# ACT counts three of the seven score tiles in the last 23 rounds of a top-k threshold search

## The reference

```python
s_idx = relu(einsum('bqhd,bkd->bqhk', qi, kidx) * (IDX_DIM ** -0.5))
score = einsum('bqhk,bqh->bqk', s_idx, w) * (IDX_HEADS ** -0.5)
score = where(mask, score, -inf)
top_val, top_idx = lax.top_k(score, topk)      # topk = 256
s = einsum('bqhd,bqkhd->bqhk', q, k[top_idx]) * (B_HEAD_DIM ** -0.5)
```

## Time and profile before

| | us |
|---|---|
| median of 3 runs | 1895.09 |
| lowest and highest | 1891.09, 1896.43 |
| the profiled execution | 1891.44 |
| its span, first to last instruction | 1889.7 |
| PE busy | 1727.5 |
| DVE busy | 1225.5 |
| ACT busy | 550.7 |
| POOL busy | 302.6 |

### The profile page before, as it was taken

The page is one execution under the profiler, slowest core; times in us unless marked ns, Lnnn a source line. Parts: engine busy times, 40 slices in busy tenths (PEclk is TensorE's granted clock), DMA queues, the critical chain, the costliest instruction groups (busy, mean ns, idle before and its releaser), DMA issues. The chain is left out here.

```text
span 1889.7 us, 21531 instructions
## 1 busy us (share of the span) xinstructions
PE 1727.5 (91%) x7518; PEld 1141.1 (60%) x7538; DVE 1225.5 (65%) x2668; ACT 550.7 (29%) x1055; POOL 302.6 (16%) x389
## 2 busy tenths in 40 slices
PE   6999999999688899999769999999996888999997
PEld 4566666788445456666345666667884454566663
DVE  3379999999754445554133799999997544455550
ACT  2286411000232233333023754200002322333330
POOL 2003422000111322211110033220001013211111
PEclk9999999999889999999979999999998899999999
DMA  5100010100502010000061000101105020000000
GB/s 170 48 23 23 23 45 23 45 24 22 195 1 90 18 40 23 23 23 23 22 181 48 23 23 23 45 25 43 45 1 195 1 89 25 32 24 23 23 23 34
DMA packets 21183, 86.26 MB, mean 46 GB/s; under 512 B 4512, under 2 KB 9120, under 8 KB 16224
## 3 DMA queue, kind: packets, MB, share of 16 engines
q1 hardware_dynamic: 21088, 84.99, 12.9%
HBM read 66.84 MB, written 18.14 MB: 45 GB/s over the span
## 5 line engine op out<-in xcount | busy, mean ns | idle before, releaser
L1235 PE MATMUL ps<-r_xn,r_w 128*128 128x384 f32 (+1 forms) x1824 | 587.2, 475 | 12.3 <-issue 7.8
L1235 PEld LDWEIGHTS ps<-r_xn,r_w 128*128 128x128 f32 x1824 | 346.7, 192 | 207.3 <-issue 21.1
L1063 DVE TENSOR_SCALAR_CACHE_REDUCE r_ix<-r_sc,smi 128x384 bf16<-128x384 f32 x434 | 405.4, 998 | 2.2
L1156 DVE TENSOR_REDUCE sm<-ps 128x1 f32<-128x384 f32 (+8 forms) x216 | 174.4, 812 | 175.1 <-PE ps L1370 87.0
L899 ACT ACTIVATE r_sc<-ps,sm 128x384 f32<-128x384 f32 (+8 forms) x216 | 169.8, 787 | 368.0 <-DVE sm L1156 367.2
L1302 PE MATMUL ps<-r_w,r_xn 128*128 128x256 f32 (+1 forms) x1152 | 251.3, 380 | 0.0
L1302 PEld LDWEIGHTS ps<-r_w,r_xn 128*128 128x128 f32 (+1 forms) x1152 | 211.4, 184 | 39.7 <-issue 5.0
L1364 PE MATMUL ps<-r_qk,r_ix 128*128 128x128 f32 (+4 forms) x608 | 157.1, 391 | 31.2 <-POOL r_ix L680 26.6
L1400 PE MATMUL ps<-r_vg,r_w 128*128 128x64 f32 (+1 forms) x1184 | 155.7, 276 | 21.7 <-DVE r_w L528 11.9
L1400 PEld LDWEIGHTS ps<-r_vg,r_w 128*128 128x128 f32 (+1 forms) x1184 | 144.6, 193 | 39.1 <-DVE r_w L491 21.7
L1364 PEld LDWEIGHTS ps<-r_qk,r_ix 128*128 128x128 f32 (+1 forms) x608 | 104.0, 197 | 88.2 <-issue 69.5
(11 more groups left out here) (175 smaller groups left out, 1721.4 us busy)
## 6 DMA issues: line engine op xcount, KB each, us to landing
r_w<-w_in SPq DMA_DIRECT2D x28, 1024.0 KB, 4.8
r_xn<-w_out SPq DMA_DIRECT2D x2, 4096.0 KB, 13.0
y<-r_res SPq DMA_DIRECT2D x16, 512.0 KB, 2.9
o_k<-r_qk SPq DMA_DIRECT2D x4, 1088.0 KB, 15.8
r_vg<-x SPq DMA_DIRECT2D x8, 512.0 KB, 10.0
r_xn<-ckT SPq DMA_DIRECT2D x2, 2048.0 KB, 7.9
r_xn<-vcache SPq DMA_DIRECT2D x2, 2048.0 KB, 13.8
o_v<-r_vg SPq DMA_DIRECT2D x4, 1024.0 KB, 17.8
```

The lines of the kernel that those rows point to most:

```text
L1063: ins = vec.tensor_scalar(unsel[t][0:rows(t), :], sc[t][0:rows(t), :], b, None, ALU.is_ge, ALU.add, accum_out=cnt[0:rows(t), c:c + 1])
L1156: vec.tensor_reduce(negm[0:r, c:c + 1], on_slot(s, w, r), X, ALU.max, negate=True)\
L1235: ins = nc.tensor.matmul(on_ring(key, cn), w[:, k, P * s + at:P * (s + 1) + at], xnT[:, k, c0:c0 + cn], start=(k == 0), stop=(k == KT - 1))
```

## The change

The tiles 6, 7 and SAMPLE (`ACT_TILES`, widths 896, 1024 and 1088) are counted by ACT in the 23 rounds of the third loop. ACT takes sign(candidate - score) over the row and sums it: below minus above. With equal values giving 0, the sum is at most `width - 512` when at least 256 scores are not below the candidate, up to the case of a score equal to it, for which `settle` makes one exact count on DVE at the candidate plus one and corrects the result. DVE counts the other four tiles, then waits for ACT's three counts (`act_counted`), compares them with `limit` in a step of its own, and goes on as before. ACT waits for each round's candidate (`cand_ready`). ACT's counts are steps of the same list as the drains: the first stands behind the 23rd projection piece after the index scores, the others behind the next 22 pieces.

```diff
+ACT_TILES = [6, 7, SAMPLE]
+DVE_TILES = [t for t in SCORED if t not in ACT_TILES]
+ND = len(DVE_TILES)
+NS = len(SCORED)
+COUNTS_AT = list(range(23, 23 + SPLITS[2]))
...
+        if done in COUNTS_AT:
+            new.append(("count", COUNTS_AT.index(done)))
...
     for u in UNITS[10:]:
         for g in range(len(TMG)):
             steps.append(("tm", u, g))
+            done += 1
+            steps += after_piece(done)
...
+                    def count_out(n):
+
+                        act.wait_ge(cand_ready, n + 1)
+                        for t in ACT_TILES:
+                            c, r = SCORED.index(t), rows(t)
+                            nc.scalar.activation(unsel[t][0:r, :], sc[t][0:r, :], ACT.Sign, scale=-1.0,
+                                                 bias=cb.bitcast(f32)[0:r, c:c + 1],
+                                                 accum_out=cnt[0:r, c:c + 1]).then_inc(act_counted, 1)
...
-                    def count(bound, last_inc):
-                        for c, t in enumerate(SCORED):
+                    def count(bound, tiles):
+                        for t in tiles:
+                            c = SCORED.index(t)
...
+                    for t in ACT_TILES:
+                        c = SCORED.index(t)
+                        vec.memset(limit[:, c - ND:c - ND + 1], float(width(t) - 2 * TOPK))
+                    vec.memset(maskf[:, 0:1], 65535.0)
+                    vec.memset(maskf[:, 1:2], 2147418112.0)
+                    link(vec.memset(maskf[:, 2:3], 65536.0))
+                    link(vec.tensor_copy(maski, maskf))
+                    link(count(0.0, SCORED))
...
+                    def search_shared(rounds):
+                        base, first = steps[0], 0
+                        per = 4
+                        with dve.Fori(0, rounds) as i:
+
+                            vec.scalar_tensor_tensor(cb, v, bitv, smask, ALU.bitwise_or, ALU.bitwise_xor)\
+                               .then_inc(cand_ready, 1)
+                            dve.wait_ge(cand_ready, i + (first + 1))
+                            count(cb.bitcast(f32), DVE_TILES).then_inc(dve_step, 1)
+                            dve.wait_ge(dve_step, i * per + (base + 1))
+                            vec.tensor_scalar(kb[:, 0:ND], cnt[:, 0:ND], float(TOPK), bitf, ALU.is_ge, ALU.mult)
+                            dve.wait_ge(act_counted, i * len(ACT_TILES) + len(ACT_TILES) * (first + 1))
+                            vec.tensor_tensor(kbf, cnt[:, ND:NS], limit, ALU.is_le).then_inc(dve_step, 1)
+                            dve.wait_ge(dve_step, i * per + (base + 2))
+                            vec.tensor_scalar(kb[:, ND:NS], kbf, bitf, None, ALU.mult).then_inc(dve_step, 1)
+                            dve.wait_ge(dve_step, i * per + (base + 3))
+                            vec.tensor_tensor(v, v, kb, ALU.bitwise_or)
...
+                    def settle():
+
+                        va, sa = v[:, ND:NS], smask[:, ND:NS]
...
+                        link(vec.tensor_tensor(cb[:, ND:NS], two, sa, ALU.bitwise_xor))
+                        link(count(cb.bitcast(f32), ACT_TILES))
+                        link(vec.tensor_scalar(ca, cnt[:, ND:NS], float(TOPK), -1.0, ALU.is_ge, ALU.mult))
...
-                    search(SPLITS[2])
+                    search_shared(SPLITS[2])
+                    settle()
```

More of the change, by code:

```diff
@@ L324, in build @@
         bitv = smi[:, 28:29]
+        limit, kbf, maskf = sm[:, 224:227], sm[:, 228:231], sm[:, 232:235]
+        sti = sb("sti", 16, i32)
+        maski = smi[:, 29:32]
         lamjunk = sb("lamjunk", CHALF)
@@ L369, in build @@
         sel_ready = sem("sel_ready")
+        cand_ready, act_counted = sem("cand_ready"), sem("act_counted")
         lam_s, lam_e, lam_ready = sem("lam_s"), sem("lam_e"), sem("lam_ready")
@@ L874, in _ @@
                             nc.scalar.activation(tall, tall, ACT.Sqrt, scale=-1.0).then_inc(root_ready, 1)
+                        elif s[0] == "count":
+                            count_out(s[1])
                         elif s[0] == "iw":
@@ L1072, in _ @@
                     vec.memset(v, 0)
-                    link(count(0.0, None))
+                    for t in ACT_TILES:
[6 more added lines that the diff above has]
+                    link(count(0.0, SCORED))
                     link(vec.tensor_scalar(smask, cnt, float(TOPK), -1.0, ALU.is_lt, ALU.mult))
@@ L1083, in search @@
                             dve.wait_ge(dve_step, i * per + (base + 1))
-                            count(cb.bitcast(f32), None).then_inc(dve_step, 1)
+                            count(cb.bitcast(f32), SCORED).then_inc(dve_step, 1)
                             dve.wait_ge(dve_step, i * per + (base + 2))
@@ L1092, in search @@
                         steps[0] = base + per * rounds
+                    def search_shared(rounds):
[14 more added lines that the diff above has]
+                            vec.tensor_tensor(v, v, kb, ALU.bitwise_or)
+                            vec.tensor_scalar(bitv, bitf, 0.5, None, ALU.mult)
+                            vec.tensor_scalar(bitf, bitf, 0.5, None, ALU.mult).then_inc(dve_step, 1)
+                            dve.wait_ge(dve_step, i * per + (base + 4))
+                        steps[0] = base + per * rounds
@@ new lines, in settle @@
+                    def settle():
+                        va, sa = v[:, ND:NS], smask[:, ND:NS]
+                        low, high, one, two, ca = (sti[:, 3 * q:3 * q + 3] for q in range(5))
+                        m16, mhi, carry = (maski[:, q:q + 1].to_broadcast([P, 3]) for q in range(3))
+                        link(vec.tensor_tensor(low, va, m16, ALU.bitwise_and))
+                        link(vec.tensor_scalar(low, low, 1.0, None, ALU.add))
+                        link(vec.tensor_tensor(one, low, carry, ALU.bitwise_and))
+                        link(vec.tensor_tensor(low, low, m16, ALU.bitwise_and))
+                        link(vec.tensor_tensor(high, va, mhi, ALU.bitwise_and))
+                        link(vec.tensor_tensor(high, high, one, ALU.add))
+                        link(vec.tensor_tensor(two, high, low, ALU.bitwise_or))
+                        link(vec.tensor_tensor(cb[:, ND:NS], two, sa, ALU.bitwise_xor))
+                        link(count(cb.bitcast(f32), ACT_TILES))
+                        link(vec.tensor_scalar(ca, cnt[:, ND:NS], float(TOPK), -1.0, ALU.is_ge, ALU.mult))
+                        link(vec.tensor_tensor(two, two, va, ALU.bitwise_xor))
+                        link(vec.tensor_tensor(two, two, ca, ALU.bitwise_and))
+                        link(vec.tensor_tensor(va, va, two, ALU.bitwise_xor))
+                        link(vec.tensor_scalar(ca, va, 8388608.0, -1.0, ALU.is_ge, ALU.mult))
+                        link(vec.tensor_tensor(va, va, ca, ALU.bitwise_and))
```

## The result

| | before | changed |
|---|---|---|
| median, us | 1893.88 (4 runs) | 1866.76 (4 runs) |
| lowest and highest | 1891.09, 1896.43 | 1862.72, 1868.75 |
| the profiled execution | 1891.44 | 1862.72 |
| its span | 1889.7 | 1860.9 |
| PE, DVE, ACT busy | 1727.5, 1225.5, 550.7 | 1722.5, 1101.5, 705.0 |

The ratio is 0.9854, with a 95% interval of 0.983 to 0.9879: the changed kernel is 27.1 us faster by the medians. DVE lost 124.0 us of work, ACT gained 154.3.

A forecast was written before the change was run, and what follows sets the result against it. It took PE's wait for POOL behind DVE's selection, 13.3 us in each layer, as the bound. Savings of 12.8 + 0.7 us per layer, 27.0 in both, gave 1864.4 from 1891.44 or 1868.1 from 1895.09, so 1867; range 1860 to 1878.

The forecast's parts named there:

- The bound: At the change to attention, PE waits for POOL, which waits for DVE's selection: 13.3 us, once in each layer.
- Part 1: Third search: sharing the counts with ACT shortens a round from 7.79 to 4.9 us, with three passes in 3.4.
- The Exp rows: ACT's Exp passes of the same widths, 1007, 1114 and 1162 ns, taken as measure for the Sign passes.
- Part 2: Projections: counts in ACT's program tie PE's banks to DVE's rounds; 4.9 against 4.88 us, stall priced at nothing.
- the slower rival: Projections: long sign passes make ACT late, banks fill and PE stands; 1933 us at passes of 6 us; chance 0.04.
- Part 3: End of selection: search ends at about 398, exact last step takes 7.5 us, selection done at about 444.
- Part 4: Start of attention: PE starts 12.8 us earlier and the unfallen clock saves 0.7 more, 13.5 us in each layer.
- The cache load: Sample tile in attention: caches land at 500.8, its first matmul moves to 509.4; 8.6 us left, no wait.
- The sum: Whole kernel: 27.0 us less in both layers, forecast 1867 us.

The follow-up runs named there:

- rounds17: The kernel before, nothing counted by ACT, with 17 instead of 23 rounds in the third loop: 1864.91 us (ratio 0.9843).
- late31: The changed kernel with its 23 counts behind pieces 31 to 53 instead of 23 to 45: 1891.68 us (ratio 0.9989 to the kernel before).
- two_more: The changed kernel with two more Sign passes on ACT in each count, into scratch: 1914.55 us (ratio 1.0108 to the kernel before).
- one_tile: The changed kernel with only the sample tile counted by ACT, DVE keeping six tiles: 1900.16 us (ratio 1.0036 to the kernel before).
- one_tile_sparse: The kernel of one_tile with the same 23 counts spread over 29 pieces: 1871.99 us (ratio 0.9892 to the kernel before).
- early17: The changed kernel with its 23 counts behind pieces 17 to 39 instead of 23 to 45: 1907.4 us (ratio 1.0067 to the kernel before).

## Why the prediction was right

*The bound.* PE's wait for POOL, twice 13.3 us, was what could be had, and it went: rounds17 got the same from a quite different relief, and late31 lost it with the full relief of DVE in place.

*Part 1, the round:* 4.9 forecast, 4.89 measured; three passes in 3.4 forecast, 3.36 measured. The Exp rows were a good measure though they read PSUM: the Sign passes take 1.04, 1.13 and 1.19 us. The Trainium skill ("ScalarE: Activation LUTs", section "Rules for kernel authors") sends simple operations to VectorE, with a figure for bf16. For these f32 passes the trace doesn't bear the rule out: ACT's 1.04 us for 896 columns stands beside DVE's 1.14.

*Part 2, the tie:* no stall, as forecast; PE waited for nothing from 277 us to its last bank. The five kernels that move or load the counts show that this was the part at risk: 2.1 us more per round, or a share of one tile, turns a gain of 27 us into a loss. A match of two paces, 4.89 and 4.88, carries the result, with banks for 14.6 us of lateness. The arithmetic of the slower rival, lateness over 18 rounds less 14.6, overstates the wait: it gives 24 us for two_more's rounds of 7.01 (16.5 and 17.5 measured) and 21 for one_tile's of 6.84 (10.0 and 15.4). What takes up the rest I haven't found.

*Part 3:* the search ended at about 396.6 (398 forecast), the last step took 6.4 us (7.5; its small steps are 14, not 15, and take 0.20 us each, not 0.26), the selection was done at 441.8 (444).

*Part 4:* forecast 12.8 + 0.7 in each layer. The wait fell by 13.31 - 0.67 = 12.64 us and, in the first layer, the distance from first to third map by 4.50 - 3.71 = 0.79: 13.43; the second layer has 12.64 and 0.78. The 0.7 had the right size but not the whole working: it counted the first map's rows only. The second map's are faster too (1.55 us before, 0.87 now), and what this adds PE gives back by waiting 2.00 us for ACT ahead of the third map, not 1.36:

```profile
501.40 1.55 PE L1364 MATMUL ps<-r_qk,r_ix 128*128 128x256 f32 x4
```
```profile
486.32 0.87 PE L1442 MATMUL ps<-r_qk,r_ix 128*128 128x256 f32 x4
```

The cache load didn't become a wait (sample tile at 507.79; 509.4 forecast, of which 1.7 is below).

*The sum:* 27.0 forecast, 27.1 by the medians. The two profiled executions differ by 28.8 in span: 26.85 at the two changes of stage, and 1.7 that has nothing to do with the change. The projections of the first layer end at 484.87 instead of 486.57, and the drain ahead of the Sqrt, before any count by ACT, stands as much earlier (232.94, not 234.64). The granted clock ahead of it was 0.96 and 1.00 in the stretches 20 to 60 and 60 to 100 us, where before had 0.91 and 0.96. In the other runs' profiles that drain stands anywhere from 231.11 to 236.10. That the median agrees to 0.2 us is therefore luck within the scatter; the mechanism and its 13.4 us per layer aren't.

## What to carry to other kernels

Read what a long helper task costs from the wait at its end, not from its length: here 1 round of 23 was worth 17.7 us, and in the first layer of one_tile_sparse 14 us of relief was as good as 53 (in its second, 10 us was not). Before work is put into the in-order program of an engine that drains another's buffers, compare the two paces and the buffers' depth: a smaller share can be worse than a large one when its partner then sets a slower pace, and the same work placed at the right distance can cost nothing.

## What the runs showed of the hardware that I had not expected

The granted clock of PE differs between executions of the same kernel, and the time goes with it. The four executions of the changed kernel had mean clocks of 0.980, 0.977, 0.974 and 0.974, and took 1862.72, 1864.83, 1868.7 and 1868.75 us, in the same order. Of the 43 executions of the kernel before that ran beside the experiments, the three fastest (1888.41 to 1889.23 us) had 0.971 to 0.973, and the three slowest (1904.32 to 1906.49) 0.961 and 0.962. That the clock is the cause of the whole scatter isn't shown by this.

An idle time of PE cost more than itself where dense matmuls followed: by the estimate above 2.8 us behind the 12.86 us in early17, against 0.76 us behind the 13.31 at the change of stage, where part of what the slow rows lose comes off PE's next wait for ACT. The clock was also below full in stretches with or behind short repeated waits: 0.91 in one_tile's first layer from 340 to 380 us, where PE idled 3.7 us of every 20. How much idle time brings it down the rows don't say: in the second layer PE idled 5.8 us of every 20 from 1280 to 1320 at a clock of 1.00, and had 0.91 from 1320 to 1360.

An f32 matmul is two rows of the trace: 27 of them made 54 rows of 0.22 us. So a map's four rows are two matmuls of the program.
